# Weighting expert rows at eviction and adding them into DRAM in a mixture-of-experts encoder

## The chip, the cores and the metric

The kernel runs on one core of a Trainium2 chip. Its time is the device time of one execution in microseconds. The figures below are the median of three timed runs and one profiled execution.

## The reference, cut to what matters

The reference is one layer of a hybrid encoder over 768 tokens (256 and 512) of width 1024 in float32: a mixer of attention and convolution, a cross-attention into memory tokens, and a mixture of experts, each followed by `h <- LN(alpha*h + f(h))`. The change is all in the last step:

```
top_v, top_i = lax.top_k(e_logits, TOP_K)                 # 2 of the 8 experts of the token's group
top_w = jax.nn.softmax(top_v, axis=-1) * p_grp
...
for e in range(N_EXPERTS):                                # 32 experts, d_expert = 256
    he = jax.nn.silu(t @ w_gate[e]) * (t @ w_up[e])
    y = y + comb[:, e:e + 1] * (he @ w_down[e])           # comb: top_w at the two chosen, else 0
...
h = _layer_norm(DEEPNORM_ALPHA * h + ff, ln3_g[l], ln3_b[l])
```

## The kernel before

The first 830 us or so (mixer, cross-attention, router) are untouched but for small constants. What matters here begins when `h` after the second norm (`LN_2`) lies in `hres` (six tiles of 128 tokens) and in a DRAM copy `h2_dram`.

**Blocks.** The 1536 (token, choice) pairs are computed in `NSB` = 22 blocks of 128 rows. A "pair" block holds two experts, one in partitions 0 to 63 and one in 64 to 127; a "one" block holds up to 128 rows of one expert. `expert_blocks()` lays them out: three pairs of the first six experts, then by the string `MIX`, where P is a pair, M one block of one expert and B two blocks of one expert. That makes 12 pair blocks and 10 single ones. Which expert stands where is decided at run time by their counts.

**TensorE.** Iteration m computes gate and up of block m (L1895 for a pair, L1898 for a single), transposes the hidden rows of block m-1 (L1907), transposes the gathered rows of block m+1 (L1872), and does the down projection of block m-1 (L1924). ScalarE and VectorE each move half of a down result from PSUM into `yo[j % 2]` (L1137, L1492).

**GpSimd.** Its queue is in program order. In iteration m it issues `gather(m + 2)`, an indirect DMA of token rows from `h2_dram` into `xg` (L836), then `scatter(m - 1)`, an indirect DMA of `yo` to `pair_dram` (L841), which has a row of its own for each (token, choice). A scatter waits for the one that used its buffer two blocks earlier, `pool.wait_ge(rows_out[j % 2], 16 * (j // 2))`. In iteration 2 it also issues the twelve scatters of `slot_table` (L881), a table that is needed only if an expert overflows its blocks.

**SyncE** loads the experts' weights: `wgu` has 6 slots (2 MB each, gate and up), `wd` has 4 (1 MB each). A slot is loaded anew once TensorE is done with the block that last used it (`load_order()`).

**The end.** `rows_out` of both buffers is awaited, `prow_used` is raised, and SyncE loads twelve tiles of 512 KB from `pair_dram` (L585). VectorE does `hres += prow * pw` twice for a tile (`add_choice`, L1527), with `pw` the router's weights, and the norm `LN_3` follows: statistics on VectorE (L640, L642), coefficients on GpSimd (L614 to L616), the scaling on ScalarE (L632), gain on GpSimd (L625), bias on VectorE (L657) and the store on SyncE (L588). Its last tile is done by VectorE alone (L650, L653).

Of the kernel before, what the change touches and what calls it, by code (L numbers as in the profile page):

```python
# [24 lines left out]
P = 128  # L25
# [26 lines left out]
MIX = "BPMPMPMPBPMPMPMPP"  # L52
GU_SLOTS, D_SLOTS = 6, 4
# [76 lines left out]

LAST_BLOCK = {n: max(j for j in range(NSB) if n in experts_of(j)) for n in range(NE)}
# [87 lines left out]
def encoder(nc, x, mem, w_slabs, lnp, rope_cos, rope_sin, q_gain, k_gain, cpar_dram, w_router, b_router,  # L219
# [4 lines left out]
    pair_dram = nc.dram_tensor("pair_rows", [2 * T, D], F32).ap()  # L224
    table_dram = nc.dram_tensor("slot_table", [T * NE, 2], I32).ap()

    with ExitStack() as ctx:
# [53 lines left out]
        wd = [scr[:, 4096:6144], ringf[:, 4096:6144], ringf[:, 6144:8192], cat[:, 4096:6144]]  # L281
        xg = [hT[:, D * n:D * (n + 1)] for n in range(2)]
# [5 lines left out]
        prow = [(cat if n % 2 == 0 else scr)[:, D * (n // 2):D * (n // 2 + 1)] for n in range(2 * NT)]  # L288
# [15 lines left out]
        lnt = sb("lnt", [P, 1])  # L304
        ssq = sb("ssq", [P, NT, NQK])
# [13 lines left out]
        sidx = [sb(f"sidx{n}", [P, 1], U32) for n in range(2)]  # L319
        ctl = sb("ctl", [1, 1 + 2 * LIST + NE], I32)  # L320
# [46 lines left out]
        tokf, pairf = rv(NT, of="fixed"), rv(NT, of="fixed")  # L367
# [33 lines left out]
        rows_out = [sem(f"rows_out{n}") for n in range(2)]  # L401
# [7 lines left out]
        prow_in = [sem(f"prow_in{n}") for n in range(2 * NT)]  # L409
        summed = sem("summed")  # L410
        prow_used, y_out, scaled = sem("prow_used"), sem("y_out"), sem("scaled")
# [33 lines left out]
        LN_3 = [LN_2[-1] + 1 + i for i in range(NT)]  # L445

        SHORT = (LN_X[0], LN_X[1], LN_2[-1], LN_3[-1])

# [6 lines left out]
        def _(sp):  # L455
# [100 lines left out]
            load_gu(4, 4)  # L556
            sp.wait_ge(scratch_done, 1)
            load_gu(5, 5)
            sp.wait_ge(order_ready, 1)
            for what, n in load_order():  # L560
# [20 lines left out]
            sp.wait_ge(prow_used, 1)  # L581
            for i in range(NT):
                for k in range(2):
                    n, r = 2 * i + k, k * T + i * P
                    sp.dma_start(prow[n], pair_dram[r:r + P, :]).then_inc(prow_in[n], 16)  # L585
            for i in range(NT):
                sp.wait_ge(ln_done, LN_3[i] + 1)
                sp.dma_start(y[i * P:(i + 1) * P, :], hres[:, i, :]).then_inc(y_out, 16)  # L588
# [3 lines left out]
        def ln_rows(n):  # L592
# [3 lines left out]
            for ns in (LN_X, LN_1, LN_2, LN_3):  # L596
                if n in ns:
                    return hres[:, ns.index(n), :], gb[:, 0, :], gb[:, 1, :]
# [1416 lines left out]
```

## Time and profile before

| | |
|---|---|
| median of 3 runs | 1151.83 us (1150.41 to 1155.04) |
| the profiled execution | 1157.94 us, span 1156.2 us, granted clock 0.918 |
| TensorE busy | 978.5 us (85% of the span) |
| VectorE, ScalarE, GpSimd busy | 427.1, 272.6, 424.6 us |
| DMA | 166.15 MB, mean 144 GB/s |
| from the first gate/up product to the last scatter's issue | 829.8 to 1105.3 us of the span |

Times of the trace are in us from the start of the span. PE is TensorE, DVE VectorE, ACT ScalarE, POOL GpSimd, SP SyncE; a q behind a name is that engine's sequencer. "Landing" is the time from a DMA's issue to the last count of its semaphore.

### The profile page before, as it was taken

Reading aid. Unit: us, or ns where it says so; the run is one execution under the profiler, and the core shown is the slowest. Engines: PE = TensorE matmul, PEld = TensorE weight load, DVE = VectorE, ACT = ScalarE, POOL = GpSimd, SP = SyncE. Lnnn points to the kernel's source line nnn. Section 1 sums busy time; section 2 is a strip of 40 time slices with the busy share of each in tenths; the row PEclk is TensorE's granted clock in tenths of the full one; section 3 lists DMA queues with packets and bytes.
Section 4 is the critical chain, followed back from the end, with each engine's and each line's share of the span. In section 5 each row is a group of like instructions: output and inputs, shape, how many; then the busy total and the mean of one; then the engine's idle time right before and its main releaser. Section 6 shows DMA issues by size and latency. Waiting matters only on the chain.

```text
span 1156.2 us, 10290 instructions
## 1 busy us (share of the span) xinstructions
PE 978.5 (85%) x3368; PEld 509.1 (44%) x3368; DVE 427.1 (37%) x702; ACT 272.6 (24%) x647; POOL 424.6 (37%) x496
## 2 busy tenths in 40 slices
PE   4899884757779998999999999995897999999910
PEld 3465442433334453444555754554643444444300
DVE  5199999566541432000000332225241112111156
ACT  2444564254421221001111430112010111111111
POOL 6688889727751542000000441120115121212037
PEclk9899997769989998999999999996598999999965
DMA  9201200120003014220420005006299799999652
GB/s 325 97 1 32 77 0 1 35 75 1 1 1 109 19 59 142 73 73 0 145 73 0 1 30 243 37 37 272 94 369 394 302 420 421 414 393 418 233 223 109
DMA packets 46234, 166.15 MB, mean 144 GB/s; under 512 B 8515, under 2 KB 13891, under 8 KB 33893
## 3 DMA queue, kind: packets, MB, share of 16 engines
q1 hardware_dynamic: 39460, 152.88, 34.3%
q0 software_dynamic: 6720, 12.60, 2.9%
q8 instruction: 28, 0.46, 0.2%
q14 instruction: 26, 0.20, 0.0%
HBM read 157.92 MB, written 18.03 MB: 152 GB/s over the span
## 4 chain that ended last, share of the span: by engine, by line
PE 68%; DVE 17%; POOL 8%; issue 4%; DMA 2%; ACT 1%; POOLq 0%; SPq 0%; DVEq 0%
PE ps L1568 34%; DVE cat L1197 11%; PE ps L1895 7%; PE ps L1924 7%; PE ps L1898 5%; POOL scr L778 4%; PE ps L1730 2%; PE ps L1654 2%; PE ps L1872 2%; PE ps L1679 2%; POOL hres L625 2%; PE ps L1577 1%; PE ps L1827 1%; PE ps L1718 1%; PE ps L1641 1%
## 5 line engine op out<-in xcount | busy, mean ns | idle before, releaser
L778 POOL TENSOR_SCALAR scr<-scr,rinv 128x256 f32<-128x256 f32 (+1 forms) x72 | 86.1, 1208 | 258.1 <-DVE rinv L1223 215.6
L1568 PE MATMUL ps<-ring,hT 128*128 128x512 f32 (+1 forms) x384 | 152.5, 558 | 23.3 <-ACT cat L990 12.9
L1568 PE MATMUL ps<-hT,ring 128*128 128x512 f32 (+1 forms) x512 | 170.7, 497 | 1.7 <-ACT hT L929 1.0
L1568 PEld LDWEIGHTS ps<-hT,ring 128*128 128x128 f32 x512 | 99.7, 195 | 71.4 <-issue 62.0
L1197 DVE SCALAR_TENSOR_TENSOR cat<-early,cpar,cat 128x512 f32<-128x512 f32 x120 | 127.5, 1063 | 4.2
L762 POOL TENSOR_TENSOR cat<-cat 128x256 f32<-128x256 f32 x120 | 114.1, 951 | 29.8 <-ACT cat L964 13.4
L1568 PEld LDWEIGHTS ps<-ring,hT 128*128 128x128 f32 x384 | 74.6, 196 | 98.8 <-issue 78.7
L1239 DVE TENSOR_REDUCE nmax<-ps 128x1 f32<-128x256 f32 x24 | 10.2, 424 | 215.3 <-PE ps L1654 215.3
L841 POOL DMA_INDIRECT pair_rows<-hT,sidx x22 | 22.0, 1001 | 182.9 <-DVE hT L1492 182.0
L1568 PE MATMUL ps<-ring,cat 128*128 128x512 f32 x192 | 83.8, 593 | 0.9 <-ACT cat L1055 0.9
L614 POOL TENSOR_SCALAR lnt<-mv 128x1 f32<-128x1 f32 x28 | 14.5, 518 | 161.0 <-DVE mv L642 160.0
L964 ACT ACTIVATE cat<-early,cpar 128x256 f32<-128x256 f32 x120 | 57.5, 506 | 43.2 <-POOL cat L762 42.7
L1924 PE MATMUL ps<-ring,memx 128*64 128x512 f32 (+1 forms) x144 | 59.9, 610 | 0.7 <-DVE memx L1482 0.7
L1568 PE MATMUL ps<-scr,ring 128*128 128x512 f32 x128 | 57.9, 616 | 0.7 <-ACT scr L1081 0.7
L1291 DVE SCALAR_TENSOR_TENSOR hres<-hres,ps 128x512 f32<-128x512 f32 x24 | 16.4, 685 | 109.3 <-PE ps L1568 109.3
L1482 DVE COPY memx<-ps 128x256 f32<-128x256 f32 x22 | 9.3, 424 | 128.4 <-PE ps L1907 124.6
L1568 PEld LDWEIGHTS ps<-ring,cat 128*128 128x128 f32 x192 | 35.9, 190 | 43.8 <-issue 43.8
L1568 PE MATMUL ps<-ring,scr 128*128 128x512 f32 x128 | 55.1, 592 | 0.0
L625 POOL TENSOR_TENSOR hres<-hres,gb 128x1024 f32<-128x1024 f32 x20 | 48.8, 2444 | 7.2 <-ACT hres L632 7.1
L632 ACT ACTIVATE hres<-hres,lnc 128x1024 f32<-128x1024 f32 x20 | 24.8, 1240 | 105.5 <-POOL lnc L616 105.3
L1718 PE MATMUL ps<-ident,scr 128*128 128x128 f32 x160 | 28.4, 304 | 21.3 <-POOL scr L778 20.3
L657 DVE TENSOR_TENSOR hres<-hres,gb 128x1024 f32<-128x1024 f32 x20 | 28.6, 1437 | 44.4 <-POOL hres L625 44.4
(267 smaller groups left out, 1447.2 us busy)
## 6 DMA issues: line engine op xcount, KB each, us to landing
ring<-w_down SPq DMA_DIRECT2D x16, 1024.0 KB
early<-w_gate SPq DMA_DIRECT2D x12, 1024.0 KB, 9.5
early<-w_up SPq DMA_DIRECT2D x12, 1024.0 KB, 13.0
ring<-w_gate SPq DMA_DIRECT2D x10, 1024.0 KB
ring<-w_up SPq DMA_DIRECT2D x10, 1024.0 KB
scr<-w_down SPq DMA_DIRECT2D x8, 1024.0 KB
cat<-w_down SPq DMA_DIRECT2D x8, 1024.0 KB
scr<-w_gate SPq DMA_DIRECT2D x5, 1024.0 KB
```

The costliest lines, as they stand in the source:

```text
L625: nc.gpsimd.tensor_tensor(rows, rows, g, ALU.mult).then_inc(ln_gain, 1)
L632: nc.scalar.activation(rows, rows, ACT.Identity, bias=lnc[:, n % 2, 1:2], scale=lnc[:, n % 2, 0:1]).then_inc(ln_hat, 1)
L657: nc.vector.tensor_tensor(rows, rows, b, ALU.add).then_inc(ln_done, 1)
L762: g.tensor_tensor(acc[:, c, 0:length], acc[:, c, 0:length], tap[n % NTAP], ALU.add).then_inc(conv_done[0], 1)
L778: g.tensor_scalar(prob[u % 4][:, 0:width], prob[u % 4][:, 0:width], rinv[:, u % 4:u % 4 + 1], None, ALU.mult).then_inc(prob_ready, 1)
L964: a.activation(tap[n % NTAP], src, ACT.Copy, scale=cpar[:, c, k:k + 1]).then_inc(taps_ready, 1)
L1197: ins = v.scalar_tensor_tensor(out=dst, in0=src, scalar=cpar[:, c, k:k + 1], in1=dst, op0=ALU.mult, op1=ALU.add)
L1568: last = t.matmul(out_of(bank), lhs(k), rhs(k), start=(k == 0), stop=(k == KC - 1))
L1718: last = t.transpose(bank[:, c * P:(c + 1) * P], prob[u % 4][:, c * P:(c + 1) * P], ident[:, :])
L1895: last = t.matmul(gu_out(64 * h, 64 * h + 64, b), xT[b][:, k, 64 * h:64 * h + 64], gu_of(n % GU_SLOTS, k), start=(k == 0), stop=(k == KC - 1))
L1898: last = t.matmul(gu_out(0, P, b), xT[b][:, k, :], gu_of(EXPERT_BLOCKS[j][1] % GU_SLOTS, k), start=(k == 0), stop=(k == KC - 1))
L1924: last = t.matmul(ps[h0:h1, 2 + n, :], hidT[b][:, k, h0:h1], w[:, k, n * 512:(n + 1) * 512], start=(k == 0), stop=(k == 1))
```

## The change

- `yo` is multiplied by the router's weight when it leaves PSUM. The weights go to DRAM (`pw_dram`, from `pw`, computed earlier), and a new indirect DMA for each block, `weigh(m)`, fetches 128 of them into `wcol`. It is issued between the gather and the scatter.
- `sum_dram` starts as alpha*h, stored from `hres` before the blocks. Each block is added to it by an indirect DMA with `compute_op=ALU.add`. Since two experts of a pair may hold the same token, a pair block is two such DMAs, each with the other half's 64 indices out of bounds. All these DMAs are in one sequence: each is issued only when the one before has landed (`SCATTERS` counts them, 34 in all).
- `hres` is then free and becomes a seventh `wgu` slot and a fifth `wd` slot.
- The twelve `slot_table` scatters go two by two into iterations 2 to 7.
- `MIX` ends in PPPM where it ended in PMPP: the last block is a single one.
- The end loads six tiles (`frow`), has nothing to add, and takes the norm's coefficients from ScalarE (Sqrt) and VectorE; GpSimd does the six gains alone.

```diff
-MIX = "BPMPMPMPBPMPMPMPP"
-GU_SLOTS, D_SLOTS = 6, 4
+MIX = "BPMPMPMPBPMPMPPPM"
+GU_SLOTS, D_SLOTS = 7, 5
...
+            for i in range(NT):
+                sp.wait_ge(scaled, i + 1)
+                sp.dma_start(sum_dram[i * P:(i + 1) * P, :], hres[:, i, :]).then_inc(sum_init, 16)
             sp.wait_ge(scratch_done, 1)
             load_gu(5, 5)
...
+            def weigh(j):
+
+                if j >= 2:
+                    pool.wait_ge(weights_in[j % 2], 16 * (j // 2))
+                row_index(j, 1, widx[j % 2], widx_ready)
+                weights_to(j % 2)
+
             def scatter(j):
 
-                if j >= 2:
-                    pool.wait_ge(rows_out[j % 2], 16 * (j // 2))
-                row_index(j, 1, sidx[j % 2], sidx_ready)
+                kind, x, y = EXPERT_BLOCKS[j]
+                n = SCATTERS[j]
+                if n:
+                    pool.wait_ge(rows_out, 16 * n)
...
                 pool.wait_ge(yo_a, j + 1)
                 pool.wait_ge(yo_d, j + 1)
-                rows_from(j % 2)
+                rows_from(j % 2, 0)
+                if kind == "pair":
+                    pool.wait_ge(rows_out, 16 * (n + 1))
+                    rows_from(j % 2, 1)
...
+                weigh(m)
                 if m >= 1:
                     scatter(m - 1)
...
+            for k in range(NT + 3):
+                if k < NT:
+                    stats3(k)
+                if 1 <= k <= NT:
+                    coef3(k - 1)
+                if k >= 3:
+                    bias3(k - 3)
```

On GpSimd, one iteration of the loop over blocks in the program before, from the gather's DMA to the scatter of a pair block (`xg` is shown as `hT`, whose memory it uses, and so is `yo`; TENSOR_LOAD reads an expert's number):

```order
L836 DMA hT<-h2_rows,gidx0 128x1024 [waits gidx_ready]
L832 TENSOR_LOAD ctl [waits rows_out1]
L832 ISA x2
L832 TENSOR_LOAD ctl
L832 ISA x2
L819 ISA
L819 TENSOR_TENSOR sidx1<-tabs 128x1
L841 DMA pair_rows<-hT,sidx1 1536x1024 [waits sidx_ready,yo_d,yo_a]
```

The same place after the change, from the weights' DMA on:

```order
L869 DMA wcol0<-pair_weights,widx0 128x1 [waits widx_ready]
L860 TENSOR_LOAD ctl [waits rows_out]
L860 ISA x2
L860 TENSOR_LOAD ctl
L860 ISA x2
L899 ISA
L899 TENSOR_TENSOR sidx0<-tabs,other 128x1
L899 ISA
L899 TENSOR_TENSOR sidx1<-tabs,other 128x1
L874 DMA sum_rows<-hT,sidx0 768x1024 [waits sidx_ready,yo_d,yo_a]
L874 DMA sum_rows<-hT,sidx1 768x1024 [waits rows_out]
```

The wait for `rows_out` ahead of the indices is now on the scatter just before, there is a second scatter behind a second such wait, and the next iteration's gather stands behind both.

On GpSimd at the end of the program, the first rows of `LN_3` before (two tiles' coefficients, and the first gain):

```order
L614 TENSOR_SCALAR lnt<-mv 128x1 [waits ln_hat,ln_stats]
L615 TENSOR_TENSOR lnc<-lnt,mhalf 128x1 [waits pool_step]
L616 TENSOR_SCALAR lnc<-mv,lnc 128x1 [waits pool_step]
L614 TENSOR_SCALAR lnt<-mv 128x1 [waits ln_done,ln_stats]
L615 TENSOR_TENSOR lnc<-lnt,mhalf 128x1 [waits pool_step]
L616 TENSOR_SCALAR lnc<-mv,lnc 128x1 [waits pool_step]
L625 TENSOR_TENSOR hres<-hres,gb 128x1024 [waits ln_hat,gb_in]
```

And all that it does there after the change (`frow` lies in `cat`), behind the branches of the overflow loop:

```order
L947 UNCONDITIONAL_BRANCH [waits rows_out]
L946 REGISTER_ALU
L946 COMPARE_AND_BRANCH
L945 UNCONDITIONAL_BRANCH
L975 TENSOR_TENSOR cat<-cat,gb 128x1024 [waits ln3_hat,gb_in]
L975 TENSOR_TENSOR cat<-cat,gb 128x1024 [waits ln3_hat] x5
```

The eighteen coefficient operations have left GpSimd; six gains are left.

## Rows read from the trace of the kernel before

**Rows 1.** Windows: length, busy us by engine, TensorE's granted clock, DMA share, GB/s.

```profile
829.80:1105.30 275.50, 261.87 (x1034) 113.29 (x1034) 53.59 (x118) 35.25 (x66) 61.70 (x95) 0.98 0.89 361
1105.30:1156.20 50.90, 0.00 (x0) 0.00 (x0) 31.73 (x37) 6.20 (x5) 29.25 (x24) 0.51 0.48 187
```

**Rows 2.** The chain in order of time, 870 to 935: start, us, what.

```profile
872.56 0.29 POOLq L832
...
873.13 0.29 POOLq L832
...
883.58 9.12 DMA hT<-h_rows,gidx
...
892.74 1.97 PE ps L1872 x8
894.71 5.21 PE ps L1924 x8
...
908.26 3.44 PE ps L1924 x8
...
918.79 0.90 PE ps L1872 x8
...
923.27 6.87 PE ps L1895 x32
...
934.90 6.87 PE ps L1898 x16
```

**Rows 3.** Waits, of TensorE (829 to 1105) and VectorE (800 to 829): total, times, longest.

```profile
PE ps L1872 <- DMA hT<-h_rows,gidx: 8.6, 1, 8.6
...
DVE tabs L1391 <- PE ps L1827: 9.0, 2, 4.7
```

**Rows 4.** Timeline of GpSimd, about the last table scatter and in a steady block.

```profile
881.56 0.97 POOL L881 DMA_INDIRECT slot_table<-tvals,slots  x1 [0.30 <-issue]
...
885.73 1.00 POOL L841 DMA_INDIRECT pair_rows<-hT,sidx  x1 [0.88 <-issue]
...
924.78 1.00 POOL L841 DMA_INDIRECT pair_rows<-hT,sidx  x1 [8.23 <-DVE hT L1492]
...
926.85 1.04 POOL L836 DMA_INDIRECT hT<-h_rows,gidx  x1 [0.82 <-POOL gidx L819]
```

**Rows 5.** Scatters to `pair_dram` from 905 to 1080: issues, and their landings.

```profile
L841 POOL DMA_INDIRECT pair_rows<-hT,sidx x15: 987/1007/1014, 913.2 to 1077.3; - x15
...
DMA to landing us min/median/max: 7.6/8.5/8.7
```

**Rows 6.** The last two scatters, issued at 1100.5 and 1105.3: landings.

```profile
DMA to landing us min/median/max: 2.6/2.6/2.6
```

**Rows 7.** Gathers from 905 to 1080: landings.

```profile
DMA to landing us min/median/max: 9.4/10.5/11.5
```

**Rows 8.** DMA view of 930 to 960: queues with packets, MB, share of 16 engines.

```profile
q1 hardware_dynamic: 1440, 10.49, 83.3%
q0 software_dynamic: 828, 2.17, 18.2%
```

**Rows 9.** Timeline of the end.

```profile
1109.04 0.34 SPq L585 DMA_DIRECT2D cat<-pair_rows  x1
...
1125.62 2.34 POOL L625 TENSOR_TENSOR hres<-hres,gb 128x1024 f32<-128x1024 f32 x1
...
1136.55 3.31 POOL L625 TENSOR_TENSOR hres<-hres,gb 128x1024 f32<-128x1024 f32 x1
...
1151.84 1.28 DVE L653 SCALAR_TENSOR_TENSOR hres<-hres,lnc,gb 128x1024 f32<-128x1024 f32 x1
```

**Rows 10.** The twelve loads of `pair_dram` at the end: landings.

```profile
DMA to landing us min/median/max: 3.5/8.4/11.9
```

**Rows 11.** Groups by line from 1110 on: count, busy us, mean ns, idle before.

```profile
L640 DVE BATCH_NORM_STATS2 stats<-hres 128x6 f32<-128x512 f32 x12 | 7.7, 680 | 0.0
...
L657 DVE TENSOR_TENSOR hres<-hres,gb 128x1024 f32<-128x1024 f32 x5 | 6.2, 1235 | 7.7 <-POOL hres L625 7.7
```

More of the change, by code:

```diff
@@ L128, in experts_of @@
     return (a, b) if kind == "pair" else (a,)
+SCATTERS = [0]
+for kind, _, _ in EXPERT_BLOCKS:
+    SCATTERS.append(SCATTERS[-1] + (2 if kind == "pair" else 1))
 LAST_BLOCK = {n: max(j for j in range(NSB) if n in experts_of(j)) for n in range(NE)}
@@ L287, in encoder @@
         hidT = [memx[:, 1024 + 256 * n:1024 + 256 * (n + 1)].rearrange("p (k t) -> p k t", k=2) for n in range(2)]
[L288 removed]
+        frow = [cat[:, D * n:D * (n + 1)] for n in range(NT)]
         hot = [hT[:, 4096 + NT * P * n:4096 + NT * P * (n + 1)].rearrange("p (t r) -> p t r", t=NT) for n in range(2)]
@@ L319, in encoder @@
         sidx = [sb(f"sidx{n}", [P, 1], U32) for n in range(2)]
+        widx = [sb(f"widx{n}", [P, 1], U32) for n in range(2)]
+        wcol = [sb(f"wcol{n}", [P, 1]) for n in range(2)]
+        other = sb("other", [P, 2], U32)
         ctl = sb("ctl", [1, 1 + 2 * LIST + NE], I32)
@@ L444, in encoder @@
         LN_2 = [LN_1[-1] + 1 + i for i in range(NT)]
-        LN_3 = [LN_2[-1] + 1 + i for i in range(NT)]
-        SHORT = (LN_X[0], LN_X[1], LN_2[-1], LN_3[-1])
+        SHORT = (LN_X[0], LN_X[1], LN_2[-1])
         def shared(n):
@@ L1153, in _ @@
                         block_act(NSB + 2 * i + b, b)
-                        block_act_out(NSB + 2 * i + b, b, NSB // 2 + i)
-            for n in LN_3:
-                act_hat(act, n)
+                        block_act_out(NSB + 2 * i + b, b, SCATTERS[NSB] + 2 * i, NSB // 2 + i + 1)
+            for k in range(NT + 1):
+                if k < NT:
+                    act.wait_ge(ln3_stats, k + 1)
+                    a.activation(lnc3[:, k, 0:1], mv3[:, k, 1:2], ACT.Sqrt, bias=epsv[:, 0:1]).then_inc(ln3_std, 1)
+                if k >= 1:
+                    act.wait_ge(ln3_coef, k)
+                    a.activation(frow[k - 1], frow[k - 1], ACT.Identity, bias=lnc3[:, k - 1, 2:3],
+                                 scale=lnc3[:, k - 1, 1:2]).then_inc(ln3_hat, 1)
         @block.vector
@@ L1369, in _ @@
             for k in range(2):
-                for n, rows in enumerate((tokf, (tokf, pairf)[k])):
+                for n, rows in enumerate((tokf, pairf[k])):
                     v.tensor_tensor(held[k][:, :, n, :], pk[k], over(rows, NE), ALU.mult)
```

196 lines of the change are left out of this document (119 added, 77 removed).

## The prediction

> **What bounds the kernel now.** I read the windows first, to find the stage that the change touches and what is busy in it. In the stage of the expert blocks, 275.5 us long, TensorE is busy for 261.9 us and the DMA engines for 0.89 of the time; in the last 50.9 us TensorE does nothing [rows 1]. So two parts are to be costed, the blocks and the end. The chain in order of time then shows the blocks: a gate/up product of 6.87 us starts every 11.63 us (923.27 to 934.90), with no wait between, and there is one hole: the transposes of block 5 start at 892.74, on the landing of a gather issued at 883.58 [rows 2]. TensorE waits 8.6 us there, its only long wait in the stage, and runs slower behind it (1.97 and 5.21 us where it else takes 0.90 and 3.44), 11.4 us in all [rows 2, 3]. The gather was late because GpSimd issued twelve table scatters ahead of it, the last at 881.56 [rows 4]. TensorE never waits for weights in this stage: the list of waits has no such row. Without the hole the blocks would take 264 us.
>
> The number that matters for the change is not in TensorE's rows. It is how long an indirect DMA takes to land. Between 905 and 1080, fifteen scatters took 7.6 to 8.7 us, median 8.5 [rows 5], and gathers 9.4 to 11.5 [rows 7]. The last two scatters, with the weight loads over, took 2.6 [rows 6]. The fifteen blocks differ in kind and in how full they are, and the landing hardly varies. So it is set by the weight stream beside it: in 930 to 960 the SyncE queue's packets take 83.3% of 16 engines, the GpSimd queue's 18.2% [rows 8]. In the kernel before nothing waits for a scatter: its buffer is needed two blocks, 23 us, later.
>
> **The blocks after the change.** Every scatter now waits for the landing of the one before. That makes one serial chain of 34 scatters: 12 pair blocks with two, 10 single ones with one. What stands between two landings I take from rows. After a landing GpSimd reads an expert's number (two reads start 0.57 us apart [rows 2]), makes the index (about 0.2) and issues 0.88 after it [rows 4]: 0.57 + 0.2 + 0.88 = 1.7 us for a single block, 2.4 for a pair with two reads and two indices, and 0.3 (estimate: the gap between back-to-back issues [rows 4]) ahead of the second half. So a pair block costs 2L + 2.7 us and a single one L + 1.7, L being the landing. TensorE needs 11.63 us for either [rows 2]. At L = 8.5 a pair takes 19.7 us and a single block 10.2, so a pair and a single block, 23.3 us of TensorE, take 29.9 us of this chain. The gather of block m+2 stands in GpSimd's queue behind both scatters of block m-2 (the order rows show it), and so TensorE comes to wait for gathers, again and again, where it waited once. ScalarE and VectorE also wait in `block_act_out` and `block_dve_out` for the scatters of two blocks earlier, with everything behind them.
>
> L falls when the chain gets slower, since the weight stream is then spread over more time. The DMA engines are busy 0.89 × 275.5 = 245 us [rows 1]. With the stage T long I take L = 2.6 + (8.5 - 2.6) × 245/T, plus what the addition costs. The trace shows no adding DMA. Below, it could cost nothing. As I see it, each row is read as well as written: the GpSimd queue moved 2.17 MB, 530 rows of 4096 bytes, in 18.2% of 16 × 30 us, 0.165 us a row [rows 8]. With 4 to 8 rows on an engine one more pass is 0.7 to 1.3 us; a half that is not full has the lower value, and I take 0.8. Above, it is a whole further trip at the landing of an idle machine, 2.6 us [rows 6]. It is nearest to the plain scatter, from the same buffer into DRAM, so I keep to 0.8.
>
> The chain starts with the first scatter, one block and a half into the stage; by two iterations of TensorE that is about 24 us. Then 33 landings and 12 × 2.7 + 9 × 1.7 = 47 us follow up to the issue of the last. T = 24 + 47 + 33 × (3.4 + 1446/T), and so T = 329 us, L = 7.8. The stage grows by 53 us (the 11.4 us of the hole are spent in this, not gained beside it). With the addition free T = 311 us (+35), with a whole further trip 371 us (+96).
>
> The Trainium skill ("DMA: Bandwidth & Descriptors", the section on the anatomy of a GpSimd-issued DMA) gives about 2.0 us plus bytes at 436 GB/s; for 64 rows of 4 KB I work out 2.6 us from it as an estimate. The trace agrees where the queues are empty (2.6) and not where the weights flow (8.5). By that page the chain would never bind; that is the first rival below.
>
> **Edits at nothing.** The table scatters, two in an iteration, are 2 × 1.28 us (0.97 and the 0.30 ahead [rows 4]) and lie between a scatter's issue and its landing; if nothing hid them, six iterations would lose 2.6 us each. `weigh` is an index and an issue, 0.2 + 0.82 + 1.04 [rows 4], in the same shadow; without it, 2.1 us a block. The router's six small operations now stand ahead of `tabled(1)`, where VectorE waits for TensorE up to 4.7 us [rows 3]; bare, they would be some 1.5 us. The six stores of `sum_dram` are 3.1 MB, by the rate of the stage's window (361 GB/s [rows 1]) 9 us of DMA, before the blocks, while TensorE builds the router's tables; the load behind them in SyncE's queue waits for the end of these tables anyway. The extra slots gain nothing, since TensorE waits for no weights. Three pairs in a row ask for six experts in 35 us, 19 MB, more than the stream brings, but the slots cover it and the blocks will be slower than that.
>
> **The end.** Before, 50.9 us from the last scatter's issue [rows 1]. After: landing 2.6 [rows 6] and 0.8 for the addition; 1.1 us to the first load (1105.3 + 2.6 to 1109.04 [rows 6, 9]); 3.5 until it lands [rows 10]. VectorE does the statistics of tiles 0 and 1 first, 2 × (1.3 + 0.2) = 3.0 by two operations of 0.68 a tile and an aggregation [rows 11]; three tiny operations for the coefficients, 0.9 as an estimate; the scaling 1.24, by the bias, which is as wide [rows 11]. Then GpSimd's six gains, 2.34 alone and 3.31 beside VectorE [rows 9], 3.1 taken: 18.6. The last bias 1.24 [rows 11], and 3.1 from VectorE's end (1153.12) to the span's end for the store [rows 9]. Sum 36.1, a gain of 14.8 us. By gains of 2.34 or 3.31 it would be 19 or 13. A single block last saves one landing of about 3 us, which this sum has in it.
>
> **Sum.** 1156.2 + 53 - 14.8 = 1194.4 us of span. The profiled execution's time is 1.7 over its span, and 6.1 over the median of the runs: 1190 us for the runs, 3.3% slower. With the addition free, and so 0.8 less in the end, the runs take 1171; with the whole further trip (+96, end -13.0) 1235.
>
> **Rivals.** *The chain doesn't bind* (faster): the landing of a half is short. Half of its 128 rows are skipped, and 2.6 us is what an empty queue gives. It decides at 3L + 4.4 = 23.3, L = 6.3, for a pair and a single block, and at 4.4 for pairs in a row. Then the hole is gained, 11.4, and 15.6 at the end: 1156.2 - 27.0, for the runs 1125. Against it: fifteen landings of at least 7.6 us, of blocks that are not all full. Chance 0.15. The whole kernel breaks even where T = 290 us, L = 6.6; a landing about there, 1146 to 1158, has 0.05. *The further trip* (slower still): the page named above says that an adding DMA reads its destination and writes it later, so nothing in it excludes this. In rows it would be a read and a write in turn; 1235, chance 0.2. *The plain scatter, the addition free*: 1171, chance 0.25. *My forecast*, 0.8 us more: 0.35. The change does what it says in each of them.
>
> **Numbers.** Forecast 1190 us. The slower cases span 1171 to 1235. The range goes down to 1148, to hold the break-even case, and up to 1235. A measurement of this kernel tells about 0.5% from no change: faster 0.15, same 0.05, slower 0.8.
>
> **What would show it.** `sum_rows` scatters that land in 6 to 9 us while weights load, and GpSimd idle ahead of the next one on that landing. Many waits of TensorE's transposes for the gather, several us each, where there was one. The stage 329 us long and DMA share near 0.75. An end of about 36 us with gains back to back on GpSimd. I am wrong if the two halves land in under 6 us, or if the addition slows the weight stream so much that TensorE waits for weights; the first turns the sign.

## The result, and the profile after

The kernel after the change takes 1211.58 us (median of four runs, 1210.36 to 1213.18), the kernel before on the same chip 1153.43 us (1150.41 to 1155.41). The ratio is 1.0507, with a 95% interval of 1.0477 to 1.0537: slower by 5.1%. The profiled execution has a span of 1211.4 us and a granted clock of 0.903.

The windows of the kernel after, of the blocks and of the end (columns as in [rows 1]):

```profile
829.80:1170.10 340.30, 278.49 (x1034) 119.35 (x1030) 53.65 (x112) 38.18 (x67) 123.22 (x163) 0.90 0.80 291
1170.10:1211.40 41.30, 0.00 (x0) 0.00 (x0) 23.79 (x36) 9.14 (x12) 16.62 (x7) 0.50 0.43 158
```

Against [rows 1] the blocks are 64.8 us longer and the end 9.6 us shorter; that is the whole difference of the spans (55.2 us). TensorE does the same 1034 matmuls, but is now busy for 0.82 of the stage where it was 0.95, and at a granted clock of 0.90 where it was 0.98. The DMA share falls from 0.89 to 0.80 as a mean, and that mean hides much: while weights flow the DMA engines are nearly full in stretches, and at the end of the stage they are mostly idle.

```profile
920.00:950.00 30.00, 25.03 (x93) 11.00 (x92) 4.39 (x8) 3.34 (x6) 9.74 (x12) 0.89 0.98 360
1130.00:1160.00 30.00, 26.47 (x102) 10.31 (x98) 5.18 (x10) 3.78 (x7) 10.95 (x16) 1.00 0.37 119
```

GpSimd is busy twice as long, which alone says nothing: in this stage it is idle for 217 us. (The window starts at 829.80 to match [rows 1]; the first product of this execution began at 829.5.)

The scatters of the kernel after, from 905 to 1080: issues (duration in ns), and their landings:

```profile
L874 POOL DMA_INDIRECT sum_rows<-hT,sidx x15: 1552/1619/1629, 911.4 to 1067.9; - x15
...
DMA to landing us min/median/max: 6.2/10.0/12.0
```

[Rows 5] had 7.6/8.5/8.7 in a like stretch. Its line counts 15 scatters, but that trace has the landing of every second one only, of 8 of the 15. The kernel e5 below has the same blocks and a trace with all of them, and there 14 scatters took 8.0 to 9.9 us, median 8.4, so the reading stands. Each landing now stands in a chain, and the lists of waits show who pays for it. First TensorE from 800 on, then GpSimd (total, times, longest):

```profile
PE ps L1951 <- DMA hT<-h_rows,gidx: 47.3, 10, 10.6
```

```profile
POOL sum_rows L874 <- DMA sum_rows<-hT,sidx: 75.8, 12, 8.6
POOL sidx L903 <- DMA sum_rows<-hT,sidx: 34.3, 8, 6.4
POOL sidx L899 <- issue: 26.8, 10, 5.7
```

Where TensorE waited once for a gather [rows 3], it waits ten times. GpSimd waits for a landing ahead of the second half of all 12 pairs, and ahead of the indices of the next block (L899 for a pair, L903 for a single one; "issue" on L899 stands where the releaser was not found). The chain in order of time shows one piece of this, for a single block and a pair:

```profile
911.41 11.99 DMA sum_rows<-hT,sidx
923.43 0.29 POOLq L860
...
925.19 10.56 DMA sum_rows<-hT,sidx
...
936.32 0.28 POOLq L860
...
938.56 1.62 POOL sum_rows L874
...
951.78 1.01 POOL slot_table L937
...
953.83 10.41 DMA hT<-h_rows,gidx
```

A landing, then 1.8 us of reading an expert's number, index and issue up to 925.19, a landing, 2.8 us up to 938.56, a landing up to 948.3, and the second half, issued at 948.59. Behind that stand two table scatters (the second is the line of 951.78) and the index for the gather of 953.83, for which TensorE waits. The table scatters hold up that gather by 2.6 us, but not the chain of landings, whose next scatter has to wait for the landing of the second half anyway.

From issue and landing of each of the 34 scatters the stage adds up: first issue at 854.1, 33 landings with a sum of 266.2 us (8.07 each), and between a landing and the next issue 3.2 us inside the twelve pairs, 27.1 ahead of pairs and 19.5 ahead of single blocks, 49.8 in all. 854.1 + 266.2 + 49.8 = 1170.1, which is the last issue. The mean of 8.07 is of two kinds of landing: the first 24, issued up to 1098, took 9.1 us in the mean, the other nine 5.3. Of the 49.8 us all but some 4 are GpSimd's own steps, about 1.8 us ahead of a single block and 2.5 ahead of a pair. So TensorE's lower clock, which could lengthen the chain only by making a scatter wait for its rows, accounts for 4 us at the most.

The landings of the six scatters from 1130 to 1165, when the last weights arrive, and of the last one (1170.1):

```profile
DMA to landing us min/median/max: 4.3/4.4/8.5
```

```profile
DMA to landing us min/median/max: 6.0/6.0/6.0
```

[Rows 6] had 2.6 for the last plain ones; of its two scatters the trace has the landing of one, and e5 has 2.6 for each of the two. The end, GpSimd's gains and two lines of VectorE from the timeline:

```profile
1184.89 2.34 POOL L975 TENSOR_TENSOR cat<-cat,gb 128x1024 f32<-128x1024 f32 x1 [13.18 <-ACT cat L1225]
1188.60 2.34 POOL L975 TENSOR_TENSOR cat<-cat,gb 128x1024 f32<-128x1024 f32 x1 [1.37 <-ACT cat L1225]
1192.30 2.34 POOL L975 TENSOR_TENSOR cat<-cat,gb 128x1024 f32<-128x1024 f32 x1 [1.37 <-ACT cat L1225]
...
1199.73 5.69 POOL L975 TENSOR_TENSOR cat<-cat,gb 128x1024 f32<-128x1024 f32 x2 [1.37 <-ACT cat L1225]
```

```profile
1185.93 1.31 DVE L1605 SCALAR_TENSOR_TENSOR lnc<-mv,lnc 128x1 f32<-128x1 f32 x1
1188.74 2.21 DVE L1605 SCALAR_TENSOR_TENSOR lnc<-mv,lnc 128x1 f32<-128x1 f32 x1
...
1199.62 0.16 DVE L1605 SCALAR_TENSOR_TENSOR lnc<-mv,lnc 128x1 f32<-128x1 f32 x1
```

The first five gains start 3.7 us apart though one lasts 2.34: each waits for ScalarE's scaling (L1225), and that for a coefficient of 128 numbers on VectorE. That operation takes 0.16 us at 1199.62, but 1.31 and 2.21 beside a gain, and then ends with it: 1185.93 + 1.31 = 1187.24 against 1184.89 + 2.34 = 1187.23, and 1190.95 against 1190.94.

### The profile page after: what moved, and what is told of

It reads as the page before. It is cut to its first block, busy times and chain, and to the rows that moved or that the text cites. A ratio compares the mean times of both kernels' runs of the same rounds, so it can differ in the third digit from the quotient of the medians.

```text
span 1211.4 us, 10463 instructions
## 1 busy us (share of the span) xinstructions
PE 995.1 (82%) x3368; PEld 514.4 (42%) x3368; DVE 420.7 (35%) x701; ACT 278.8 (23%) x655; POOL 475.1 (39%) x553
## 4 chain that ended last, share of the span: by engine, by line
PE 48%; DVE 17%; DMA 13%; issue 11%; POOL 8%; POOLq 2%; ACT 1%; SPq 0%; DVEq 0%; ACTq 0%
PE ps L1647 32%; DVE cat L1267 10%; DMA sum_rows<-hT,sidx 10%; POOL scr L804 3%; DMA hT<-h_rows,gidx 2%; PE ps L1809 2%; PE ps L1733 2%; PE ps L1758 2%; POOL sum_rows L874 2%; POOLq L860 1%; PE ps L1656 1%; PE ps L1974 1%; PE ps L1906 1%; PE ps L1797 1%; PE ps L2003 1%
## 5 line engine op out<-in xcount | busy, mean ns | idle before, releaser
L874 POOL DMA_INDIRECT sum_rows<-hT,sidx x34 | 54.2, 1593 | 105.1 <-DMA sum_rows<-hT,sidx 75.8
L1951 PE MATMUL ps<-ident,hT 128*128 128x128 f32 x176 | 31.7, 338 | 47.3 <-DMA hT<-h_rows,gidx 47.3
L634 POOL TENSOR_SCALAR lnt<-mv 128x1 f32<-128x1 f32 x22 | 11.4, 516 | 147.3 <-DVE mv L662 146.7
L2003 PE MATMUL ps<-ring,memx 128*64 128x512 f32 (+1 forms) x112 | 53.9, 672 | 0.7 <-DVE memx L1552 0.7
L1951 PEld LDWEIGHTS ps<-ident,hT 128*128 128x128 f32 x176 | 27.0, 205 | 50.1 <-DMA hT<-h_rows,gidx 49.2
L1797 PE MATMUL ps<-ident,scr 128*128 128x128 f32 x160 | 28.2, 303 | 21.4 <-POOL scr L804 20.5
L1974 PE MATMUL ps<-early,hT 128*64 128x512 f32 x128 | 44.4, 628 | 0.8 <-ACT hT L1187 0.8
```

What stands on the lines that cost most here:

```text
L874: g.indirect_dma_start(sum_dram, bass.IndirectOffsetOnAxis(ap=sidx[n][:, :], axis=0), yo[b], None, bounds_check=last_token, oob_is_err=Fal ...
L1797: last = t.transpose(bank[:, c * P:(c + 1) * P], prob[u % 4][:, c * P:(c + 1) * P], ident[:, :])
L1951: last = t.transpose(ps[:, 4 + c // 4, c % 4 * P:(c % 4 + 1) * P], xg[b][:, c:D:KC], ident[:, :])
L1974: last = t.matmul(gu_out(64 * h, 64 * h + 64, b), xT[b][:, k, 64 * h:64 * h + 64], gu_of(n % GU_SLOTS, k), start=(k == 0), stop=(k == KC - 1))
L2003: last = t.matmul(ps[h0:h1, 2 + n, :], hidT[b][:, k, h0:h1], w[:, k, n * 512:(n + 1) * 512], start=(k == 0), stop=(k == 1))
```

## The experiments

Theory: the chain of landings sets the pace of the blocks; everything else in the stage lies in its shadow. The rivals are the price of the addition as such, the gather's place in the queue, GpSimd's own work, the weights' slots, and the scatters' DMA work. Profiled executions differ by some 6 us in when the stage begins (the first scatter is issued between 848.3 and 854.1), so I compare the chain's length, from the first scatter's issue to the last: 251.2 us before (854.1 to 1105.3), 316.0 after (854.1 to 1170.1). There is one trace for each kernel. The kernels after, e11 and e12 are the same up to the last scatter, and their chains are 316.0, 318.7 and 321.2 us, so a difference of 5 us between two chains tells nothing. The ratio of each kernel is to the kernel before, run on the same chip.

| kernel | chain, us | end, us | median, us | ratio, 95% interval |
|---|---|---|---|---|
| after | 316.0 | 41.3 | 1211.58 | 1.0507 (1.0477 to 1.0537) |
| e1, plain scatters | 284.8 | 40.1 | 1180.06 | 1.0191 (1.0158 to 1.0225) |
| e2, gather first | 315.8 | 41.1 | 1209.88 | 1.0474 (1.0446 to 1.0501) |
| e3, no weight stream | 248.9 | 41.7 | 1141.01 | 0.9875 (0.985 to 0.99) |
| e4, two sums | 270.7 | 46.9 | 1172.33 | 1.0147 (1.0111 to 1.0182) |
| e7, old slots | 319.5 | 41.3 | 1213.10 | 1.0503 (1.0482 to 1.0524) |
| e8, old order of blocks | 321.9 | 39.7 | 1215.58 | 1.0521 (1.0497 to 1.0545) |
| e9, no weights' fetch | 315.6 | 40.9 | 1208.60 | 1.0450 (1.0408 to 1.0493) |
| e11, coefficient in another form | 318.7 | 38.5 | 1214.09 | 1.0524 (1.0491 to 1.0556) |
| e12, gains on VectorE | 321.2 | 37.4 | 1209.91 | 1.0483 (1.0449 to 1.0517) |
| e5, before with table split | 247.7 | 50.5 | 1151.28 | 0.9960 (0.9947 to 0.9973) |
| e6, e5 and the new norm | 245.9 | 51.0 | 1148.67 | 0.9961 (0.9944 to 0.9979) |
| e10, e5 and B earlier | 245.8 | 51.2 | 1149.97 | 0.9949 (0.993 to 0.9968) |

### e1: the same chain, without the addition

```diff
-    bounds_check=last_token, oob_is_err=False, compute_op=ALU.add).then_inc(rows_out, 16)
+    bounds_check=last_token, oob_is_err=False).then_inc(rows_out, 16)
```

> The kernel after, with the add operation taken from the 34 scatters: each overwrites its rows, so the sum over choices and alpha*h are missing. The chain of landings, its waits and its order stay. Theory 1 (the chain of landings sets the pace, the addition is only one term of a landing): with the idle landing of a plain scatter, 2.6 us, in place of the 3.8 us that the mean of 8.07 us leaves for it, the sum 24 + 50 + 33 x (2.6 + 1446/T) gives a stage of about 312 us (340 after) and a run of about 1182 us. Theory 2 (the addition itself, by its reads or by what it does to the weight stream, is what costs): the stage goes back to 264 to 275 us and the run to 1140 or 1150. Theory 3 (the addition is free): stage 340, run 1211 as after.

The blocks of e1, and its scatters from 905 to 1080:

```profile
829.80:1138.90 309.10, 270.18 (x1034) 116.39 (x1030) 53.65 (x112) 37.69 (x67) 102.50 (x164) 0.94 0.82 321
```

```profile
L874 POOL DMA_INDIRECT sum_rows<-hT,sidx x18: 980/1017/1032, 906.3 to 1074.4; - x18
...
DMA to landing us min/median/max: 3.5/8.5/10.1
```

The stage is 309.1 us where 312 was expected, the run 1180 where 1182 was. The median landing is that of the plain scatters of [rows 5], 8.5, and an issue is 1.0 us again instead of 1.6. So the addition costs 31 us of the stage, about half of what it grew by; the waits alone, with plain scatters, still leave the kernel 1.9% slower than before. Theories 2 and 3 are out. That 309 came so near to 312 is in part luck: the landings add up to 221.9 us and what lies between a landing and the next issue to 62.9, where the sum had 239 and 50. With shorter landings the chain has to wait for TensorE's products in places (up to 6.5 us between a landing and the next issue).

### e2: the gather ahead of the scatters

```diff
                 rows_from(j % 2, 0)
+                between()
...
+            gather(2)
+            weigh(0)
+            gather(3)
+            weigh(1)
             for m in range(NSB):
-                if m + 2 < NSB:
-                    gather(m + 2)
-                weigh(m)
...
+                def ahead():
...
+                    if m + 3 < NSB:
+                        gather(m + 3)
+                    if m + 1 < NSB:
+                        weigh(m + 1)
                 if m >= 1:
-                    scatter(m - 1)
+                    scatter(m - 1, ahead)
```

`between()` is the function `ahead` that `scatter` is given.

> The kernel after, with gather(m+3) and weigh(m+1) issued right after the indices and before a block's first scatter waits for its rows, so that no gather stands behind the two scatters of its own iteration. The chain of landings is unchanged. Theory 1 (the chain sets the pace, TensorE's waits for gathers are only where its slack is spent): stage 335 to 345 us, the run within 6 us of 1211; TensorE's waits move from the gathers to ScalarE and VectorE. Theory 2 (the gather's place behind the scatters in GpSimd's queue is the cause): the waits at the transposes, 47 us, go away and the run falls to 1165 to 1175.

TensorE's waits for gathers in e2:

```profile
PE ps L1961 <- DMA hT<-h_rows,gidx: 49.5, 8, 14.0
```

The chain is 315.8 us, as before the edit, which speaks for theory 1. But theory 1 also said that the waits would move to ScalarE and VectorE, and they did not: TensorE waits for gathers as long as before, in fewer and longer pieces (8 and up to 14.0 us, against 10 and 10.6). Why they stayed at the gathers isn't shown. A likely reason is that GpSimd's whole queue runs as late as the chain, so that an issue moved ahead by one wait is late again a block further on. What the run shows is that the gather's place isn't what the stage's length hangs on.

### e3: no weight stream

```diff
-            for what, n in load_order():
+            for what, n in []:
```

with TensorE's waits for weights set to the first load of each slot.

> The kernel after without the expert weight loads after the first fill of the slots (later experts are computed with stale weights). All DMAs of GpSimd and the chain stay. Theory 1 (a landing is long because of the weight stream beside it): landings of 4.3 to 4.5 us throughout, a pair block 2 x 4.4 + 2.9 = 11.7 us of chain and a single one 6.2, so TensorE's 11.63 sets the pace again: stage 264 to 280 us, run 1135 to 1152. Theory 2 (an adding indirect DMA that scatters rows is slow by itself, or by its wait): landings stay above 7 us, stage above 320, run above 1190.

The adding scatters of e3 from 905 to 1080, and TensorE's waits for gathers:

```profile
L874 POOL DMA_INDIRECT sum_rows<-hT,sidx x22: 1552/1610/1626, 912.5 to 1075.7; - x22
...
DMA to landing us min/median/max: 4.3/5.8/6.2
```

```profile
PE ps L1951 <- DMA hT<-h_rows,gidx: 2.1, 2, 1.9
```

Without the stream a landing is 5.8 us instead of 10.0, and the chain no longer binds: 248.9 us. The stage is 273.5 us (824.4 to 1097.9) with TensorE busy for 261.8 of them, as in the kernel before; the run is 1.2% faster than that, mostly by its shorter end. GpSimd is busy for 123.3 us of this stage as it is in the kernel after (123.2), so its own work isn't what makes the stage long. Theory 2, over 7 us by itself, is out. But I had expected 4.3 to 4.5 throughout, and that was wrong for full blocks. I read the landings one by one, beside the number of rows that each scatter has by the reference's routing of its inputs. Scatters of up to 22 rows landed in 4.1 to 4.6 us, those of 36 to 128 rows in 5.5 to 6.2 (one, early, in 8.3). The mean over the first 33 is 5.33.

### e4: two sums, 22 steps in the chain instead of 34

```diff
+    sum2_dram = nc.dram_tensor("sum_rows2", [T, D], F32).ap()
...
                 if kind == "pair":
-                    pool.wait_ge(rows_out, 16 * (n + 1))
-                    rows_from(j % 2, 1)
+                    rows_from(j % 2, 1, sum2_dram)
...
-                a.activation(hres[:, i, :], hres[:, i, :], ACT.Copy, scale=ALPHA).then_inc(scaled, 1)
+                a.activation(hres[:, i, :], hres[:, i, :], ACT.Copy, scale=ALPHA / 2).then_inc(scaled, 1)
...
+                v.tensor_tensor(frow[k], frow[k], srow[k], ALU.add).then_inc(both_in, 1)
```

> The kernel after with a second DRAM sum: the second half of a pair block is added to that one, so the two halves of a pair needn't wait for each other. Each sum starts as alpha*h/2; the end loads twelve tiles and VectorE adds them two by two. The chain has then 22 steps, one for each block, instead of 34. Theory 1 (number of landings in series times landing): a pair step is one landing of 8.5 to 9.5 us plus 1.6 us for the second issue plus 2.4, 12.5 to 13.5 us, a single one 10 to 11, against 11.63 of TensorE: stage 275 to 295 us. The end grows by 8 to 12 us (six more loads of 512 KB and six additions). Run 1155 to 1180. Theory 2 (not the number of waits but the DMA work of 34 adding scatters is what costs): the stage stays at 340, and the run goes to 1215 to 1225.

The scatters of e4 (the whole program), and TensorE's waits for gathers:

```profile
L879 POOL DMA_INDIRECT sum_rows<-hT,sidx x34: 1538/1604/1631, 851.5 to 1122.2; - x34
```

```profile
PE ps L1957 <- DMA hT<-h_rows,gidx: 20.1, 12, 3.9
```

The same 34 adding scatters, with twelve waits fewer: the chain is 45.3 us shorter, though a landing takes longer (9.2 us in the mean of the first 33 instead of 8.1, two at a time in the pairs). The stage is 295.4 us, at the upper edge of what was expected. TensorE now waits in twelve small pieces. The end is 46.9 us instead of 41.3, 5.6 us more, less than the 8 to 12 us that I had allowed. It is the number of landings in series that costs, and the DMA work of the scatters isn't it.

### e9: nothing of the weights' fetch

```diff
-                weigh(m)
...
-                act.wait_ge(weights_in[b], 16 * weighed)
...
-                dve.wait_ge(weights_in[b], 16 * weighed)
```

> The kernel after without the weights' indirect DMA of each block and without the waits for it (the rows are scaled with what the column holds, so that the weighting is left out). It takes about 2 us of GpSimd a block out of the shadow of the landings. Theory 1 (the chain of landings sets the pace, the work between issue and landing is free): the run within 4 us of 1211. Theory 2 (GpSimd's queue is the bound): 22 x 2.1 = 46 us less, 1165.

The scatters of e9:

```profile
L874 POOL DMA_INDIRECT sum_rows<-hT,sidx x34: 1530/1582/1628, 853.3 to 1168.9; - x34
```

The chain is 315.6 us (316.0 after). The fetch lies in the shadow, as forecast; GpSimd's own work isn't the bound, or the run would be near 1165.

### e7 and e8: the slots and the order of the last blocks

```diff
-GU_SLOTS, D_SLOTS = 7, 5
+GU_SLOTS, D_SLOTS = 6, 4
```

> The kernel after with the old weight slots, 6 and 4, so that the residual's memory is not reused. Theory 1 (TensorE waits for no weights, the chain sets the pace): run within 4 us of 1211, the stage 337 to 343 us. Theory 2 (the extra slots matter now, or start more of the stream early and so raise the first landings): a difference of over 6 us either way, with waits of TensorE for weights in the list.

```diff
-MIX = "BPMPMPMPBPMPMPPPM"
+MIX = "BPMPMPMPBPMPMPMPP"
```

> The kernel after with the old order of the last blocks (a pair block last, a single one before two pairs earlier). The number of landings is the same, 34. Theory 1: the last TensorE product is followed by two landings instead of one, so the run is slower by one idle landing and the index, 4 to 6 us, 1215 to 1218. Theory 2 (the chain is so far behind TensorE that the order doesn't matter): within 3 us of 1211.

The slots change nothing that a measurement tells: 1.0503 against 1.0507, and TensorE waits for no weights in either. With a pair last the chain is 5.9 us longer, as one landing more behind TensorE's last product would make it, and the end 1.6 us shorter, since the last half has few rows and lands in 4.4 us instead of 6.0. That makes 4.3 us by the profile, but the chain of e12, with the blocks of the kernel after, is as long as that of e8 (321.2 and 321.9), and the intervals of the runs overlap. So an effect of the order isn't shown.

### e5, e6 and e10: what the kernel before gains from the parts that stand alone

In e5 the twelve table scatters go two by two into iterations 2 to 7, and nothing else changes.

```diff
+                if 2 <= m < 2 + NT:
...
-                        for i in range(NT):
-                            g.indirect_dma_start(table_dram, bass.IndirectOffsetOnAxis(ap=slots[:, k, i:i + 1], axis=0),
-                                                 tvals[:, i, k, :], None, bounds_check=T * NE - 1,
+                        g.indirect_dma_start(table_dram, bass.IndirectOffsetOnAxis(ap=slots[:, k, m - 2:m - 1], axis=0),
+                                             tvals[:, m - 2, k, :], None, bounds_check=T * NE - 1,
```

> The kernel before with one part of the change: the twelve scatters of the overflow table are issued two by two in iterations 2 to 7 instead of all in iteration 2. Nothing else. Theory 1 (the hole of 11.4 us at block 5 is the gather behind the twelve scatters): TensorE's wait of 8.6 us at the transposes goes, the stage is 264 us (275.5 before), the run 1142. Theory 2 (the weight stream or another gather takes the hole's place): the wait reappears elsewhere, the run within 4 us of the kernel before.

The hole at block 5 is gone (a wait of 1.3 us is left at 884.4), and some 90 us later there is another. The chain of e5 in order of time, then the landing of the one load of `w_down` issued at 959.9:

```profile
977.86 0.90 PE ps L1872 x8
978.76 5.00 issue
983.76 6.54 PE ps L1924 x16
```

```profile
L534 SPq DMA_DIRECT2D ring<-w_down x1: 333/333/333, 959.9 to 959.9; - x1
...
DMA to landing us min/median/max: 23.7/23.7/23.7
```

The down product stands still for 5.0 us and starts 0.2 us after that load has landed (959.9 + 23.7 = 983.6), then takes 6.54 us instead of 3.6: TensorE had stood still for 5.0 us, and its granted clock from 983.8 to 990.2 was 0.54, near the lower of its two levels; from 920 to 950 it was 1.00. Together that is 7.9 us. The profile calls the wait "issue", because its releaser was not found. The kernel before has a small wait of the same name in the same product (at 989.3), whose weights' landings its trace lacks:

```profile
PE ps L1924 <- issue: 1.4, 1, 1.4
```

The window ahead of the 5.0 us wait in e5 shows what the load of 23.7 us had beside it:

```profile
950.00:980.00 30.00, 28.76 (x113) 13.23 (x111) 5.71 (x11) 4.14 (x8) 6.39 (x12) 1.00 1.02 422
```

The DMA engines were full all that time. The run gained 0.4% where I had expected 1%, within the 4 us of theory 2: the weight stream took most of the hole's place. In the kernel before, too, the DMA share is 1.02 from 920 to 980, at 421 to 422 GB/s, but behind the hole, from 890 to 920, it is 0.78 where e5 has 1.00: the hole had let the stream get ahead.

In e10, e5 with the second expert of two blocks placed earlier:

```diff
-MIX = "BPMPMPMPBPMPMPMPP"
+MIX = "BPMPMPBPMPMPMPMPP"
```

> The kernel before with the split table scatters and the second expert of two blocks placed two blocks earlier in MIX (BPMPMPBPMPMPMPMPP), so that the first half of the stage asks for fewer experts' weights. Where the table scatters alone were split, 11.4 us of hole were gone and a 5.0 us wait of a down product came at 978.8, with w_down landing 23.7 us after its issue. Theory 1 (the weight stream took the hole's place: 417 to 422 GB/s from 860 to 980): with two blocks of one expert before that place the wait goes or falls under 1.5 us, the stage is 264 to 267 us, the run 1143 to 1146. Theory 2 (the wait has to do with that block or place itself): it stays at 5 us and the run at 1151. If the stream only runs out later, a wait of the same size shows behind 1010.

The chain of e10, about the largest wait:

```profile
1054.88 0.90 PE ps L1872 x8
1055.78 3.88 issue
```

At 978.8 nothing waits any more, but at 1055.8 there is a wait of 3.9 us, which ends 0.2 us after a load of `w_down` issued at 1036.9 has landed (22.6 us). That is the third case of the expectation: the stream only runs out later. The stage is 270.1 us (271.8 in e5), and the medians of e5 and e10 can't be told apart. Against the kernel before each is faster, by 0.4 and 0.5%, with intervals that exclude 1; with e6 below they are the best kernels here that compute the whole.

> The kernel before with two parts of the change: the split table scatters, and the new norm at the end (statistics on VectorE, coefficients on ScalarE and VectorE, gains alone on GpSimd), here behind the twelve loads and the weighting of the two rows, which stay. Theory 1 (part of the shorter end comes from the norm's form): 11.4 us from the hole, and 2 to 6 us of the end, run 1136 to 1142. Theory 2 (the end is bound by VectorE's twelve weighted additions and the loads, which land until 11.9 us): the end stays at 50 us or grows by the coefficients on VectorE, run 1142 to 1147.

e6 adds the new norm behind the old twelve loads:

```diff
-            norms(LN_3)
+            for i in range(NT):
+                pool.wait_ge(ln3_hat, i + 1)
+                g.tensor_tensor(hres[:, i, :], hres[:, i, :], gb[:, 0, :], ALU.mult).then_inc(ln3_gain, 1)
...
+                a.activation(lnc3[:, k, 0:1], mv3[:, k, 1:2], ACT.Sqrt, bias=epsv[:, 0:1]).then_inc(ln3_std, 1)
...
```

Its end is 51.0 us against 50.5 in e5, VectorE being busy for 36.93 us of it against 31.72. So theory 2 held for the end, and the norm's form gives nothing as long as the twelve loads and the weighting stand ahead of it. The run, 1148.7 us, is slower than both theories said (1136 to 1142, 1142 to 1147), since both had counted on the whole hole. That the 9.6 us which the changed kernel saves at the end come from the six loads and twelve weighted additions that fall away follows only by elimination: the changed kernel with the old norm was not run.

### e11 and e12: why the gains were not back to back

```diff
-                v.scalar_tensor_tensor(out=lnc3[:, k, 2:3], in0=mv3[:, k, 0:1], scalar=-1.0, in1=lnc3[:, k, 1:2],
-                                       op0=ALU.mult, op1=ALU.mult).then_inc(ln3_coef, 1)
+                v.tensor_scalar(out=lnc3[:, k, 2:3], in0=mv3[:, k, 0:1], scalar1=lnc3[:, k, 1:2], scalar2=-1.0,
+                                op0=ALU.mult, op1=ALU.mult).then_inc(ln3_coef, 1)
```

> The kernel after with one small operation of the norm at the end in another form: minus mean times reciprocal deviation (128x1) as a tensor_scalar with one tensor operand, instead of a scalar_tensor_tensor with two. In the trace after, the latter took 1.31, 2.21, 1.07 and 1.08 us beside a gain on GpSimd and ended within 0.02 us of the gain's end each time (0.16 without one), while reciprocals and statistics ran on beside the gains. Theory 1 (VectorE operations with two tensor operands wait for GpSimd's): the new form takes 0.2 us or less, the scaling on ScalarE is no longer tied to the end of the gain before, gains start every 2.4 to 3.6 us instead of 3.7, the end is 1 to 4 us shorter than 41.3. Theory 2 (any VectorE write beside a gain waits, or small operations are late for another reason): it still takes over 1 us, cadence 3.7, end 41.3.

The timeline of e11:

```profile
1185.66 7.95 POOL L975 TENSOR_TENSOR cat<-cat,gb 128x1024 f32<-128x1024 f32 x3 [13.14 <-ACT cat L1225]
...
1186.42 0.21 DVE L1605 TENSOR_SCALAR lnc<-mv,lnc 128x1 f32<-128x1 f32 x1
...
1188.13 0.21 DVE L1605 TENSOR_SCALAR lnc<-mv,lnc 128x1 f32<-128x1 f32 x1
1188.26 3.15 DVE L1611 TENSOR_TENSOR cat<-cat,gb 128x1024 f32<-128x1024 f32 x1
```

The coefficient takes 0.21 us beside a gain, three gains run back to back in 7.95 us, and the end is 38.5 us instead of 41.3. What is now held up beside the gains is the bias addition, 3.15 us instead of 1.21.

```diff
-                g.tensor_tensor(frow[i], frow[i], gb[:, 0, :], ALU.mult).then_inc(ln3_gain, 1)
...
+                v.tensor_tensor(frow[k], frow[k], gb[:, 0, :], ALU.mult).then_inc(ln3_gain, 1)
```

> The kernel after with the six gains of the last norm on VectorE instead of GpSimd. Theory 1 (a gain on GpSimd, 2.34 us, keeps VectorE's additions from running, so that the two engines take turns): on VectorE a gain is 1.24 us, VectorE's row at the end is 6 x 1.5 of statistics, 6 x 0.3 of coefficients and 12 x 1.3, 26.4 us from the first tile at 1180.3 to 1206.7 and 3 us for the store, an end of 39 to 40 us against 41.3. Theory 2 (the two engines do work side by side, GpSimd's six gains being 14 us of work taken off VectorE): the end grows by 3 to 7 us.

The end of e12:

```profile
1169.90:1207.30 37.40, 0.00 (x0) 0.00 (x0) 23.81 (x42) 8.85 (x12) 1.54 (x1) 0.50 0.47 174
```

It is 3.9 us shorter than in the kernel after, and 1.6 shorter than the least that was expected, with six operations more on VectorE and nothing but a scatter's issue on GpSimd. VectorE is busy no longer than before (23.81 against 23.79 us), since its coefficients and additions no longer stand waiting (the small operation is 0.16 us each time). Both experiments speak for theory 1. In the runs these 3 to 4 us don't show, the intervals overlap with that of the kernel after; the chains of these two executions happened to be 2.7 and 5.2 us longer.

## Why the prediction was right, and where its sums were off

**The mechanism held.** The forecast was 1190 us with a range of 1148 to 1235; it took 1211.6. The chain of 34 scatters is what sets the blocks' time: removing waits (e4) shortens it by 45 us, removing the stream beside it (e3) brings TensorE's pace back, and the gather's place (e2), the slots (e7) and the weights' fetch (e9) don't account for it. Of the signs that the prediction named, the many waits for gathers and GpSimd idle on landings came as said. Others did not: beside the weights the landings were 6.2 to 12.0 us, median 10.0, where it had said 6 to 9, and the DMA share was 0.80 where it had said 0.75. The stage was forecast at 329 us and is 340.3: the chain's start was right (24 us, measured 24.3), the work between landings 49.8 us instead of 47, and the 33 landings 266.2 instead of 257.4 (8.07 each instead of 7.8).

**The landing was near by two errors against each other.** That part of the hit was luck. The sum took 3.4 us for an adding scatter on an idle machine, 2.6 and 0.8 for the addition, with the reason "It is nearest to the plain scatter". On an idle machine it measured 4.1 to 4.6 us for few rows and 5.5 to 6.2 for 36 and more, 5.33 in the mean (e3): for the addition that is 1.8 us over the 2.6 of [rows 6] with few rows, and 2.8 us for the last block, whose landing was 6.0 with the addition and 3.2 without (e1). Of each, 0.6 us is the longer issue on GpSimd (1.6 for 1.0). For the last block that is above the prediction's upper bound, the whole further trip of 2.6, and with few rows it is still more than twice the 0.8. The stream's part, which the formula put at 4.4 us, was 2.7 (8.07 - 5.33). With the idle landing alone put right, the prediction's own formula comes to its case of the further trip (5.2 us), 1235 us. [Rows 6] held the landing of one scatter, with 16 rows of 128 by the reference's routing, and told nothing of full ones. In place, among the weights, the addition lengthened the mean of the first 33 landings from 6.72 (e1) to 8.07. The formula also held the DMA engines' work at 245 us. By share times length it was 272 us after and 253 in e1, for the same bytes (99 MB) in all three kernels: the addition keeps the 16 engines busy for some 19 us, by estimate 0.20 us for each of the 1536 rows on one engine, near the 0.165 of the prediction's further pass. A plain chain was forecast at 311 us of stage and measured 309.1, again with landings shorter than said (6.72 for 7.25) and more between them (62.9 us for 47). The Trainium skill's figure for a GpSimd-issued DMA ("DMA: Bandwidth & Descriptors", the section on the anatomy of one), by which the prediction's first rival would have come true, met the trace only for plain scatters of few rows on an idle machine (2.6 us); beside the weight stream the median was 8.5 us in e1.

**The break-even held.** With landings of 5.33 us, under the 6.3 at which the prediction let the chain decide, TensorE set the pace again (e3). The rival "the chain doesn't bind" failed on the landings, as the rows against it said (8 recorded landings and not the fifteen that it counts).

**The end was forecast at 36.1 us and took 41.3.** The last landing was 6.0 us instead of 3.4: +2.6. Between it and the first gain things went 1.0 us faster. The step that failed is "Then GpSimd's six gains, 2.34 alone and 3.31 beside VectorE [rows 9], 3.1 taken: 18.6", with the sign "gains back to back on GpSimd": from the first gain to the end of the last it was 20.5 us (1184.89 to 1205.42), and the last bias, 1.0, and the store, 0.7, were longer than taken. I had read GpSimd's gain as slowed by VectorE (3.31 in [rows 9]), and not that VectorE's operations would be held up by GpSimd's and hold up ScalarE behind them. e11 shows it. The Trainium skill ("SBUF — State Buffer", the section on who interferes with whom) says that a VectorE instruction with two SBUF inputs contends with a GpSimd instruction that reads SBUF, and that one with at most one such input, outside VectorE's two-port modes, doesn't. The traces of the kernel after and of e11 agree (2.21 against 0.21 us).

**From the span to the runs.** I took 4.4 us off the span, since the profiled execution of before was 6.1 us over its median. After the change the profiled execution (1213.18 us) is 1.6 over its median, so the runs are 0.2 above the span. 11.8 us of the stage (the sum has 275.5 + 53 = 328.5), 5.2 of the end and these 4.6 are the 21.6 us by which 1190 was too low.

**The hole was no gain to be had in full.** "Without the hole the blocks would take 264 us" was wrong: e5 took 271.8 us of stage and e10 270.1. TensorE's list of waits had no row that names weights, but it had the 1.4 us of "issue" at a down product, and in e5 the wait of that name ended 0.2 us after weights had landed. What should have warned me, too, is the share of the DMA engines beside it ([rows 8], 83.3 and 18.2% together). In the changed kernel this made no difference, as the chain was slower than either. It speaks against the fastest rival, 1125 us, which counts the whole hole as gained.

**The edits at nothing.** The weights' fetch (e9) and the slots (e7) cost or gave nothing measurable; for the order of the last blocks, which the prediction put at about 3 us, the profile of e8 has 4.3, not clear of the spread between executions. The placing of the table scatters in the changed kernel was not tried apart.

## What to carry to other kernels

A transfer that nobody waits for costs its bandwidth; put a wait behind it and it costs its latency, as loaded as the machine is at that point. Before chaining transfers, multiply their number by the landing in that stage (here 34 times 8 us, against 262 us of TensorE's work), take the landing from a kind of transfer that is measured, and look first for a way to have fewer in series: a second destination gave back 45 of 65 us, while moving other work around in the same queue gave nothing. And a wait that is not in the list, or has no name there, may be covered by another one: before counting a hole as a gain, look at what runs at its limit beside it.

## What the runs showed of the hardware

- An indirect DMA that adds took 1.6 us to issue on GpSimd (1.0 plain), and without the weight stream (e3) landed in 4.1 to 4.6 us with up to 22 rows of 4 KB and in 5.5 to 6.2 us with 36 to 128 rows, but for one early landing of 8.3. Between 36 and 128 rows the number mattered little: 5.8 us in the mean up to 60 rows, 6.0 from 73 on.
- The rows that its bounds skip saved landing time only where few were left: in e3 the halves of 43 to 60 rows took 5.7 to 6.0 us and the two scatters of 128 rows 5.9 and 6.2.
- The addition kept the DMA engines busy longer for the same bytes: 0.80 of 340.3 us against 0.82 of 309.1 in e1.
- A VectorE operation on 128x1 numbers with two tensor operands took up to 2.21 us beside a 2.34 us gain on GpSimd and ended with it; with one tensor operand it took 0.21. Reciprocals (0.11 to 0.15) and statistics (1.2 to 1.3 for two) were not held up.
- The core's DMA engines moved 417 and 422 GB/s in the windows 920 to 950 and 950 to 980 of e5, 84% of the bytes by SyncE's queue, which loads the weights, and a load of 1 MB issued in it took 23.7 us to land.
